# GpSimd takes the low part of each expert's last down panel in the experts' tiles

## What is computed

```
    g_sel = jnp.argmax(g_logits, axis=-1)
    ...
    top_p, top_i = lax.top_k(e_prob, TOP_K_IN_GROUP)
    ...
    for e in range(N_EXPERTS):
        h = jax.nn.silu(xt @ w_gate[e]) * (xt @ w_up[e])
        y = y + combine[:, e:e + 1] * (h @ w_down[e]).astype(f32)
```

## Time and profile before

| | us |
|---|---|
| median of 3 runs | 2767.51 |
| lowest and highest | 2763.73, 2769.31 |
| profiled execution, its own time | 2762.17 |
| its span in the trace | 2760.3 |
| TensorE busy in the span | 2625.8 (95%) |
| VectorE busy | 1322.6 (48%) |
| ScalarE busy | 972.7 (35%) |
| GpSimd busy | 195.3 (7%) |

### The profile page before, as it was taken

The page is one execution under the profiler, slowest core; times in us unless marked ns, Lnnn a source line. Parts: engine busy times, 40 slices in busy tenths (PEclk is TensorE's granted clock), DMA queues, the critical chain, the costliest instruction groups (busy, mean ns, idle before and its releaser), DMA issues.

```text
span 2760.3 us, 31117 instructions
## 1 busy us (share of the span) xinstructions
PE 2625.8 (95%) x12644; PEld 2098.3 (76%) x12644; DVE 1322.6 (48%) x1732; ACT 972.7 (35%) x1291; POOL 195.3 (7%) x151
## 2 busy tenths in 40 slices
PE   7996994999999999899999999999999998999998
PEld 6875772788887777578888888888877766888886
DVE  5354995534345343274443454444533435544444
ACT  5344883322233132543222242222412245422222
POOL 0001112400002300010000000000050001000000
PEclk9997996999999999999999999999999999999999
DMA  4117983222223221032222232222322202222222
GB/s 134 62 54 252 394 338 123 92 99 92 93 85 126 80 75 57 8 113 98 94 92 99 81 103 99 92 99 88 118 84 77 77 16 77 92 99 92 99 90 71
DMA packets 86687, 290.82 MB, mean 105 GB/s; under 512 B 10174, under 2 KB 15230, under 8 KB 86286
## 3 DMA queue, kind: packets, MB, share of 16 engines
q1 hardware_dynamic: 79406, 262.48, 28.3%
q0 software_dynamic: 6560, 24.22, 2.3%
q10 hardware_dynamic: 576, 2.10, 0.2%
HBM read 276.17 MB, written 12.58 MB: 105 GB/s over the span
## 4 chain that ended last, share of the span: by engine, by line
PE 89%; DVE 4%; ACT 3%; issue 2%; DMA 1%; POOL 0%; SPq 0%; POOLq 0%; DVEq 0%; ACTq 0%
PE bank_l L446 76%; PE bank_l L1189 2%; PE bank_s L1189 2%; DVE w_lo L420 1%; PE bank_t L446 1%; PE bank_s L1825 1%; ACT w_hi L415 1%; PE bank_t L1720 1%; PE bank_s L1841 1%; PE bank_o L1856 1%; PE bank_s L1845 1%; ACT xt_hi_tile L1249 1%; PE bank_t L1768 0%; DVE part L2104 0%; POOL square_sum L1588 0%
## 5 line engine op out<-in xcount | busy, mean ns | idle before, releaser
L446 PE MATMUL bank_l<-xg_hi,w_hi 128*128 128x512 f32 (+1 forms) x2192 | 876.4, 400 | 21.3 <-DVE w_lo L420 14.9
L446 PE MATMUL bank_l<-xg_lo,w_hi 128*128 128x512 f32 (+1 forms) x2192 | 862.6, 394 | 0.0
L446 PE MATMUL bank_l<-xg_hi,w_lo 128*128 128x512 f32 (+1 forms) x2192 | 856.8, 391 | 0.0
L420 DVE TENSOR_TENSOR w_lo<-w_raw,w_hi 128x1024 fp32r<-128x1024 f32 (+2 forms) x441 | 521.0, 1182 | 260.8 <-ACT w_hi L415 259.7
L415 ACT ACTIVATE w_hi<-w_raw 128x1024 fp32r<-128x1024 f32 (+2 forms) x441 | 435.4, 988 | 473.9 <-PE bank_l L446 457.0
L446 PEld LDWEIGHTS bank_l<-xg_hi,w_hi 128*128 128x128 f32 x2192 | 415.8, 190 | 128.1 <-issue 15.8
L446 PEld LDWEIGHTS bank_l<-xg_lo,w_hi 128*128 128x128 f32 x2192 | 415.7, 190 | 97.3 <-issue 8.4
L446 PEld LDWEIGHTS bank_l<-xg_hi,w_lo 128*128 128x128 f32 x2192 | 416.5, 190 | 89.6
L446 PE MATMUL bank_l<-hid_hi_ff,w_lo 128*128 128x512 f32 x704 | 278.8, 396 | 0.0
L446 PE MATMUL bank_l<-hid_hi_ff,w_hi 128*128 128x512 f32 x704 | 278.8, 396 | 0.0
L446 PE MATMUL bank_l<-hid_lo_ff,w_hi 128*128 128x512 f32 x704 | 278.8, 396 | 0.0
(11 more groups left out here) (334 smaller groups left out, 2520.5 us busy)
## 6 DMA issues: line engine op xcount, KB each, us to landing
w_raw<-in_ff_gate SPq DMA_DIRECT2D x88, 512.0 KB, 3.4
w_raw<-in_ff_up SPq DMA_DIRECT2D x88, 512.0 KB, 3.4
expert_raw<-in_experts SPq DMA_DIRECT2D x81, 512.0 KB, 6.6
w_raw<-in_in SPq DMA_DIRECT2D x80, 512.0 KB, 3.5
w_raw<-in_ff_down SPq DMA_DIRECT2D x64, 512.0 KB, 3.5
w_raw<-in_out SPq DMA_DIRECT2D x24, 512.0 KB, 3.5
w_raw<-in_ff_down SPq DMA_DIRECT2D x32, 384.0 KB, 3.0
y_rows<-y_slot_tile POOLq DMA_DIRECT2D x16, 512.0 KB, 6.6
```

The costliest lines, as they stand in the source:

```text
L420: dve.tensor_tensor(w_lo[:, i % SPLIT, 0:kc * cols], panel_memory(i), w_hi[:, i % SPLIT, 0:kc * cols].bitcast(F32), ALU.subtract).then_inc ...
L446: done = pe.matmul(dst, w[:, i % SPLIT, c * cols:(c + 1) * cols], moving, start=c == 0 and n == 0, stop=c == kc - 1 and n == 2)
```

## The change

The low part of panel (i, 5) of each tile i is computed by GpSimd instead of VectorE: 16 of the 96 panels of the experts. It raises a semaphore of its own, `panel_lo_pool`, and everybody who waits for such a panel's low part (TensorE ahead of the product, SyncE ahead of the load that reuses the slot) waits for that one. `rest_ahead` skips these panels on VectorE. In `tiles_pool` the new instruction stands behind the gather of tile i + 2 and ahead of the wait for the output copies of tile i - 1. The overflow tiles (for experts with more than 128 tokens), which have their own panels, are not touched.

```
+        panel_lo_pool = steps("panel_lo_pool")
...
-                sp.wait_ge(*panel_lo.upto(before_in_slot[i]))
+                sp.wait_ge(*lo_of(before_in_slot[i]))
...
+        def by_pool(i):
+
+            return order[i][0] == "experts" and order[i][1][1] == TILE_PANELS - 1
+
+        def lo_of(i):
+            return (panel_lo_pool if by_pool(i) else panel_lo).upto(i)
...
-                              w_hi[:, i % SPLIT, 0:kc * cols].bitcast(F32), ALU.subtract).then_inc(*panel_lo.done(i))
+            dve.tensor_tensor(w_lo[:, i % SPLIT, 0:kc * cols], panel_memory(i), w_hi[:, i % SPLIT, 0:kc * cols].bitcast(F32),
+                              ALU.subtract).then_inc(*(panel_lo_pool if by_pool(i) else panel_lo).done(i))
...
-                rest_of_panel(dve, rested[0])
+                if not by_pool(rested[0]):
+                    rest_of_panel(dve, rested[0])
...
-            pe.wait_ge(*panel_lo.upto(i))
+            pe.wait_ge(*lo_of(i))
...
+                if i and run.first_tile == 0:
+                    rest_of_panel(pool, panel_of["experts", (i - 1, TILE_PANELS - 1)])
...
-            tiles_pe(pe, tile_run, lambda i, j: panel_lo.upto(panel_of["experts", (i, j)]),
+            tiles_pe(pe, tile_run, lambda i, j: lo_of(panel_of["experts", (i, j)]),
```

More of the change, by code:

```diff
@@ L417, in rest_of_panel @@
         def rest_of_panel(dve, i):
+            dve.wait_ge(*panel_hi.upto(i))
             kc, cols = panel_shape(i)
-            dve.wait_ge(*panel_hi.upto(i))
-            dve.tensor_tensor(w_lo[:, i % SPLIT, 0:kc * cols], panel_memory(i),
-                              w_hi[:, i % SPLIT, 0:kc * cols].bitcast(F32), ALU.subtract).then_inc(*panel_lo.done(i))
+            dve.tensor_tensor(w_lo[:, i % SPLIT, 0:kc * cols], panel_memory(i), w_hi[:, i % SPLIT, 0:kc * cols].bitcast(F32),
+                              ALU.subtract).then_inc(*(panel_lo_pool if by_pool(i) else panel_lo).done(i))
         rounded, rested = [0], [0]
```

## The result

The changed kernel takes 2775.3 us (median of 8 runs, 2769.6 to 2781.7), the kernel before 2765.6 us (8 runs, 2755.1 to 2769.3). The ratio is 1.0036, 95% interval 1.0021 to 1.0050: some 10 us slower. The profiled execution has a span of 2770.1 us against 2760.3, + 9.8.

What follows compares the result with a forecast made beforehand. ScalarE's high parts and TensorE, not VectorE, were taken as the bound. 14 rounds at 0.91 us (12.7) plus 0.6 gave 13.3 us: 2775.5 from the profiled 2762.2, 2781 as median; range 2777 to 2785 (72%), outer 2770 to 2796.

Steps and rivals of the forecast that it cites:

- What bounds the kernel: Experts' rounds: ScalarE's high parts and TensorE set the pace; VectorE's removed instruction is not on the path.
- Gain 0: VectorE without the low part of (i - 1, 5): the time saved becomes idle time, gain 0 us.
- The price of GpSimd's instruction: Low part of 1024 columns on GpSimd: 2.30 us behind VectorE's end, range 2.07 to 2.58.
- rival 1: GpSimd's subtraction is slow through rounded output and two tiles, 3.13 us at the far end: 2790 to 2800 us; 12%.
- Lateness: TensorE starts panel (i - 1, 5) 0.83 us later, plus 0.08 for restarting from rest: 0.91 us a round, 14 rounds.
- the handover: From GpSimd's end to TensorE's first matmul of (i - 1, 5): 0.16 us, as from VectorE's low part.
- The last tiles: GpSimd blocks VectorE's low part of (15, 4), delaying the first feed-forward load: + 0.6 us; (15, 5) is hidden.
- The sum: Whole change: 12.7 us from 14 rounds plus 0.6 us at the last tiles, 13.3 us slower.
- Exclusion: GpSimd waits for VectorE's two-SBUF-input instruction to end, and the reverse; without it GpSimd starts some 0.25 us earlier each round.
- No change: GpSimd is short enough, at most 1.47 us behind VectorE's end at 338.99, so the time stays 2767.5 us; 9%.
- Faster: VectorE is the bound; relieving it removes TensorE's 0.31 us wait and 0.08 restart: 5.5 us, about 2762; 4%.
- The clock: TensorE's granted clock falls in part to 1.2 GHz through longer rests in the rounds: 2795 us or more; 3%.

Runs made afterwards that it cites:

- the run with the idle GpSimd instruction: Kernel before plus a GpSimd 128x1024 subtraction on a spare tile behind the high part of (i, 5), result unused: rounds 11.53 us, 2791.0 us, single execution.
- the other order: Kernel before, with ScalarE's and VectorE's parts of (i - 1, 4) ahead of the next tile's tokens: rounds 9.72 us, 2759.2 us, ratio 0.9987.

## Why the prediction was right

**What bounds the kernel.** Right. VectorE, 93% busy, was not on the path: without its instruction the rounds stay at 10.01 us, and a mere change of ScalarE's and VectorE's order shortens them with VectorE's load unchanged. What told it was that VectorE's low part of (i - 1, 4) began 0.02 us behind the end of its high part.

**Gain 0.** Right, by the run in which nobody computes the low part.

**The price of GpSimd's instruction.** Forecast 2.30 us behind VectorE's end, doubled from the earlier trace rows; measured 2.25. The range of 2.07 to 2.58 held it, with the rounded format as output and two tiles as inputs: no slow form (rival 1). Doubling a row of 512 columns came out because there is next to nothing fixed in this distance (1.14 us at 512, 2.25 at 1024); the prediction had no row that showed this, so to that extent it was luck.

**Lateness.** Forecast 0.83 + 0.08 = 0.91 us a round, measured 0.69 + 0.11 = 0.80 (0.79 from the rounds). The term mis-sized most is the handover: I took the 0.16 us from VectorE's end to TensorE's start of (i - 1, 4), and from GpSimd's end to (i - 1, 5) it is 0.06. The runs show that this goes by the panel and not by the engine. At (i - 1, 5) it is 0.06 us from VectorE too, in the run with half of the panel each (335.15 to 335.21). At (i - 1, 4) it is 0.15 us from VectorE in the changed kernel (343.36 to 343.51), and 0.15 us from GpSimd as well, where GpSimd has that panel (336.27 + 2.41 = 338.68 to 338.83):

```profile
336.27 2.41 POOL L428 TENSOR_TENSOR w_lo<-expert_raw,w_hi 128x1024 fp32r<-128x1024 f32 x1 [0.19 <-ACT w_hi L423]
```
```profile
338.83 0.48 PE L1198 MATMUL bank_s<-w_hi,ht_hi_tile 128*128 128x512 f32 x1
```

Why the two panels differ was not tried. GpSimd's instruction itself was 0.05 us shorter, and the restart 0.03 us dearer. Over 14 rounds this makes 11.1 us instead of 12.7.

**The last tiles.** Forecast + 0.6 us, from the load of the first feed-forward panel on. In the changed kernel it is issued at

```profile
432.20 0.33 SPq L409 DMA_DIRECT2D w_raw<-in_ff_gate  x1
```

against 420.93: 11.3 us later, and 11.6 with the first transposes 0.3 us earlier in this execution. The 14 rounds explain 11.1 of them, so 0.5 us remain, by the wait that the prediction named. VectorE's last copy moved from 428.7 to 439.8, 11.1 us, so there only 11.4 - 11.1 = 0.3 us remain: from the issue of that load to ScalarE's high part of it passed 4.00 us instead of 4.27. That the low part of (15, 5) is hidden held for this panel, though TensorE waited 1.2 us for it: VectorE's last copy stands behind two low parts of feed-forward panels in both kernels. The run with (i, 4) on GpSimd shows what the same queue costs without that cover, 5 us.

**The sum.** 11.4 us in the tiles against 13.3; the medians differ by 9.7, the interval is 5.8 to 13.8. The span grew by 9.8 us, 1.3 less than VectorE's last copy moved. From there to the first gather behind the experts 0.9 us are won back (it starts at 448.75 us, 7.7 us behind the start of the last store; before at 438.54, 8.6 us behind it), and the two attention stages together are 0.4 us shorter, one by 3.1 us and the other longer by 2.6, which has nothing to do with the change (below). The rest of the distance to the forecast median lies in its base: 2767.5 us was the median of three runs, and that of eight is 2765.6.

**Exclusion.** That GpSimd and VectorE exclude each other, where VectorE reads two SBUF tiles, is right, and the run with the idle GpSimd instruction shows it without any data between them. VectorE's "hidden", with one input in PSUM, took its usual 0.42 us while GpSimd worked (343.66 to 344.08 in the changed kernel). Its price for GpSimd was too high: not 0.25 us a round but 0.09 (2.47 us with 0.22 us of waiting against 2.38 without), so 0.13 us of the wait coincided with something that GpSimd's instruction takes anyway. For VectorE it costs 0.9 us in the low part of (i + 1, 0), drawn out to about 2.1 us as forecast and covered as forecast (0.5 us ahead of TensorE's need).

**The rivals.** A slow form: refuted (2.25 us, not 3.13). No change: refuted, but its point of decision was right (1.47 us forecast, 1.57 measured). Faster: refuted; its 5.5 us for a round without the wait was nearly right (4.1 us by the other order), but VectorE's load was not what the wait hung on. The clock: refuted, 1.00 over the rounds as before.

## What to carry to other kernels

A busy share of 93% does not make an engine the bound: look whether its instruction on the chain starts when its queue comes free or when its input is ready. When an instruction goes to a slower engine, compare the time between its input and its consumer with the duration there, and count what the two engines do to each other. Here it paid to put the critical instruction ahead of a neighbour in its own queue (about -4 us), and it cost 10 us to move an uncritical one to an idle engine.

## What the runs showed of the hardware

- A GpSimd instruction that was issued during a VectorE instruction ran ahead of the next VectorE instruction, which stood ready (twice: the divided panel and the idle instruction). VectorE lost 1.1 and 1.7 us by it. A VectorE instruction with one input in PSUM lost nothing beside GpSimd's (0.42 us as before).
- A GpSimd subtraction with two SBUF tensors as inputs and the rounded format as output ended 1.14, 1.71 and 2.25 us behind VectorE's release for 512, 768 and 1024 columns: 2.2 ns a column and next to nothing fixed. With both inputs and a float32 output in one tile 1024 columns took 1.98 us in all, after a like wait for VectorE, against 2.47; whether the tiles or the output format make the difference was not tried.
- From GpSimd's or VectorE's end to TensorE's start 0.06 us passed at one panel and 0.15 us at another, whichever engine it was.
- Between the same two instructions around the first attention stage, executions differ by up to 8 us, although no edit touches it. ScalarE's first `xg_hi` ahead of it and behind it, in the kernel before, the changed one, and the one with the divided panel:

```profile
820.71 0.71 ACT L491 ACTIVATE xg_hi<-x,gains 128x512 fp32r<-128x512 f32 x1
1205.47 0.71 ACT L491 ACTIVATE xg_hi<-x,gains 128x512 fp32r<-128x512 f32 x1
```
```profile
830.87 0.71 ACT L500 ACTIVATE xg_hi<-x,gains 128x512 fp32r<-128x512 f32 x1
1212.56 0.71 ACT L500 ACTIVATE xg_hi<-x,gains 128x512 fp32r<-128x512 f32 x1
```
```profile
829.37 0.71 ACT L505 ACTIVATE xg_hi<-x,gains 128x512 fp32r<-128x512 f32 x1
1219.04 0.71 ACT L505 ACTIVATE xg_hi<-x,gains 128x512 fp32r<-128x512 f32 x1
```

  That is 384.8, 381.7 and 389.7 us, with a granted clock of 0.96, 1.00 and 0.89 between 1100 and 1180 us. This is as much as most of the effects here, which is why the rounds of one stage were compared and not only totals.
